# Two of GLA's eight v and gate half pieces move from the recurrences into the turns and the chunk matrices

## The reference, cut to what matters

```python
def even_mixer(x, w_in, ...):
    p = x @ w_in
    p_gla, p_rw = p[..., :GLA_IN], p[..., GLA_IN:]
    gq, gk, gv, gg, glr = jnp.split(p_gla, GLA_OFFSETS, axis=-1)      # 256, 256, 512, 512, 16 columns
    log_a = jax.nn.log_sigmoid((glr @ gla_gate_w2 + gla_gate_b)) / GLA_TAU
    o_a = gla_chunked(gq * GLA_DK ** -0.5, gk, gv, log_a)              # 4 heads
    o_a = rms_norm(o_a, gla_norm_g) * jax.nn.silu(gg)
    ...
    y = rwkv7_scan(r, decay, k, v, -kk, kk * a)                        # 8 heads
    ...
    return jnp.concatenate([o_a, o_b], axis=-1) @ w_out
```

## Time and profile before

| what | us |
|---|---|
| median of 3 runs | 1191.01 |
| lowest, highest | 1189.79, 1195.37 |
| the profiled execution | 1193.05 |
| its span in the trace | 1191.1 |
| TensorE busy in it | 1101.9 |

### The profile page before, as it was taken

One profiled execution on the slowest core, in us unless ns is written; L12 is line 12 of the kernel. 1 busy time (PEld: TensorE's weight loads), 2 busy tenths in 40 slices (PEclk: granted clock), 3 DMA queues, 4 the chain that ended last, 5 costly groups with the idle time before them and its releaser, 6 DMA issues.

```text
span 1191.1 us, 16934 instructions
## 1 busy us (share of the span) xinstructions
PE 1101.9 (93%) x7036; PEld 973.0 (82%) x7036; DVE 727.1 (61%) x1002; ACT 516.9 (43%) x734; POOL 136.8 (11%) x153
## 2 busy tenths in 40 slices
PE   5999899988999999889889899999789997999997
PEld 4798899866999988667667899998678777999885
DVE  3476875576666675745774676675655556666342
ACT  3452242244344433515663544433355656555331
POOL 1004653114000000500001300000200000000000
PEclk9897899989999999889999899999979997999999
DMA  9332002223886787254772587777434332665540
GB/s 290 107 123 73 1 2 71 72 92 120 304 278 231 249 279 251 75 175 154 107 216 83 198 284 260 248 247 283 141 123 128 105 107 72 185 194 189 195 157 36
DMA packets 113438, 193.68 MB, mean 163 GB/s; under 512 B 4658, under 2 KB 85057, under 8 KB 113234
## 3 DMA queue, kind: packets, MB, share of 16 engines
q1 hardware_dynamic: 109698, 179.66, 45.3%
q0 software_dynamic: 3248, 11.83, 4.5%
q10 hardware_dynamic: 416, 1.11, 0.2%
HBM read 188.39 MB, written 4.19 MB: 162 GB/s over the span
## 4 chain that ended last, share of the span: by engine, by line
PE 82%; DVE 9%; ACT 4%; issue 2%; SPq 1%; DMA 1%; POOL 0%; ACTq 0%; DVEq 0%
PE ps L415 22%; PE ps L416 22%; PE ps L417 22%; PE ps L1965 2%; PE ps L1950 2%; PE ps L1179 2%; DVE ARR L399 1%; PE ps L1943 1%; PE ps L1189 1%; PE ps L1416 1%; PE ps L1123 1%; PE ps L481 1%; ACT ARR L386 1%; DMA ring<-in_ffn_w_gate_up_dram 1%; DVE XL L551 1%
## 5 line engine op out<-in xcount | busy, mean ns | idle before, releaser
L399 DVE TENSOR_TENSOR ARR<-ring,ARR 128x2048 fp32r<-128x2048 f32 (+1 forms) x143 | 321.8, 2256 | 209.8 <-ACT ARR L386 209.8
L415 PE MATMUL ps<-XH,ARR 128*128 128x256 f32 x1232 | 355.9, 289 | 14.2 <-DVE XL L551 7.5
L386 ACT ACTIVATE ARR<-ring 128x2048 fp32r<-128x2048 f32 (+1 forms) x143 | 266.9, 1874 | 201.2 <-PE ps L417 141.5
L416 PE MATMUL ps<-XL,ARR 128*128 128x256 f32 x1232 | 352.9, 286 | 0.0
L417 PE MATMUL ps<-XH,ARR 128*128 128x256 f32 x1232 | 352.6, 286 | 0.0
L415 PEld LDWEIGHTS ps<-XH,ARR 128*128 128x128 f32 x1232 | 239.4, 194 | 19.7 <-issue 17.2
L416 PEld LDWEIGHTS ps<-XL,ARR 128*128 128x128 f32 x1232 | 239.4, 194 | 0.1
L417 PEld LDWEIGHTS ps<-XH,ARR 128*128 128x128 f32 x1232 | 239.3, 194 | 0.0
L415 PE MATMUL ps<-ARR 128*128 128x512 f32 x420 | 171.0, 407 | 8.8 <-DVE ARR L503 4.6
L416 PE MATMUL ps<-ARR 128*128 128x512 f32 x420 | 167.6, 399 | 0.0
L417 PE MATMUL ps<-ARR 128*128 128x512 f32 x420 | 167.4, 399 | 0.0
(11 more groups left out here) (336 smaller groups left out, 1281.9 us busy)
## 6 DMA issues: line engine op xcount, KB each, us to landing
ring<-in_ffn_w_gate_up_dram SPq DMA_DIRECT2D x44, 1024.0 KB, 5.9
ring<-in_w_dram SPq DMA_DIRECT2D x32, 1024.0 KB, 5.2
ring<-in_w_ada_dram SPq DMA_DIRECT2D x24, 1024.0 KB, 5.3
ring<-in_ffn_w_down_dram SPq DMA_DIRECT2D x22, 1024.0 KB, 5.0
ring<-in_even_w_in_dram SPq DMA_DIRECT2D x13, 1024.0 KB, 5.8
ring<-in_w_in_dram SPq DMA_DIRECT2D x9, 1024.0 KB, 5.3
ring<-in_mla_w_q_b_dram SPq DMA_DIRECT2D x6, 768.0 KB, 6.5
ring<-in_even_w_out_dram SPq DMA_DIRECT2D x4, 1024.0 KB, 5.0
```

The costliest lines, as they stand in the source:

```text
L386: e.activation(split(i)[0], raw(i), ACT.Copy).then_inc(*up("hi", ("hi", i)))
L399: e.tensor_tensor(lo, raw(i), hi.bitcast(F32), ALU.subtract).then_inc(*up("lo", ("lo", i), ("raw free", i)))
L415: e.matmul(out, lhs[0], rhs[0], start=first, stop=False)
L416: e.matmul(out, lhs[0], rhs[1], start=False, stop=False)
```

## The change

Half 0 goes into the turns and half 1 into the chunk matrices, on all three engines that touch them.

- PE: half 0 between the transposes `kb` and the product `bonus`; half 1 behind the sixth of the 16 products of the chunk matrices. In the recurrences each later half moves up, so that no half is left behind levels 3 and 5.
- ACT splits halves 0 and 1 ahead of all of the turns, and half 2 behind them. DVE does its part of halves 0 and 1 ahead of the copy of `bonus`, and half 2 where half 0 was.
- Half 1 gets a place in SBUF of its own, and both first halves wait for the last use of `qk`'s weights.
- Banks 6 and 7 are held from the turns on, so that turns, matrices and inverse go round 6 banks. DVE reads `la` after the first and second mask, no longer after the second and third.
- ACT copies v out of its banks at level 1 in place of level 3.

No instruction is added or dropped.

```diff
-        VG_SLOT = 4 * [halves(mats + 6144, 1024), (place(gg_at, 1024, of=ARR), lo_half)]
+        VG_SLOT = [halves(mats + 6144, 1024), halves(mats + 4096, 1024)] + 3 * [
+            halves(mats + 6144, 1024), (place(gg_at, 1024, of=ARR), lo_half)]
...
-            if k == 0:
+            if k < 2:
                 e.wait_ge(*at(("used", place_of["qk", 2])))
-            elif k == 1:
+            elif k == 3:
                 e.wait_ge(*at(("p done", 6, NG - 1)))
...
         def pe_turns(e):
+            banks.n = 6
...
                 k.then_inc(*up("gates", ("full", ("kb", w))))
+            pe_vg_half(e, 0)
             b = bank(e, "bonus")
...
                 k.then_inc(*up("mats", ("full", ("m", s))))
+                if s == 5:
+                    pe_vg_half(e, 1)
...
-                if s in (1, 2):
-                    t = s - 1
+                if s in (0, 1):
+                    t = s
                     e.wait_ge(*at(("abs", t)))
...
                 elif lv == 4:
-                    dve_vg_half(e, 0)
+                    dve_vg_half(e, 2)
...
                     if j == 0 and step == 4:
-                        pe_vg_half(e, 3)
+                        pe_vg_half(e, 5)
...
-        VG_BEHIND = {0: 0, 1: 1, 2: 2, 3: 4, 4: 5, 5: 6}
-        VG_SPLIT = {-1: [1], 0: [2], 1: [3], 2: [4], 3: [5, 6], 4: [7]}
+        VG_BEHIND = {0: 2, 1: 3, 2: 4, 4: 6}
+        VG_SPLIT = {-1: [3], 0: [4], 1: [5], 2: [6], 4: [7]}
 
         def pe_recurrences(e):
-            banks.n = 6
...
-                if lv == 3:
+                if lv == 1:
                     act_vg(e, 0)
...
             act_qk(e)
+            act_vg_half(e, 0)
+            act_vg_half(e, 1)
             act_turns(e)
-            act_vg_half(e, 0)
+            act_vg_half(e, 2)
...
             dve_operands(e, 3)
+            dve_vg_half(e, 0)
+            dve_vg_half(e, 1)
             dve_turns(e)
```

## The result

| | median, us | lowest to highest | runs | mean granted clock, as us at 0.50 |
|---|---|---|---|---|
| before | 1191.47 | 1189.70 to 1195.37 | 10 | 121 |
| changed | 1199.18 | 1193.52 to 1202.71 | 10 | 135 |

What follows compares the result with a forecast made beforehand. PE was taken as the bound, busy 93% of the span, with DVE's masks setting the matrices' end. Matrices +8.3 and recurrences -6.25 gave +2.05 on 1191.01, so 1193.1 us, range 1186.0 to 1199.0.

Steps and rivals of the forecast that it cites:

- Part 1: Turns: half 0 is ready behind kb, wait nought, at worst 0.2 us; bonus and the matrices start 2.90 us later.
- The bank order: Matrices: products 1 and 2 each wait for a bank round trip, 2.27 us at full clock, 3.18 at low.
- Half 1: Matrices, behind product 5: costs PE 2.90 to 5.42 us, taken as 4.1; DVE runs dry, ten masks left.
- The matrices as a whole: Turns and matrices: last mask ends at 135.3 instead of 126.99, +8.3 us; +4.4 all at full clock, +11.5 all low.
- Rival 1: Matrices: bank waits and half 1 are hidden, only half 0 is paid; -3.35, 1187.7 us; chance 0.14.
- Rival 4: Turns and matrices: half 0 or 1 not ready when PE comes, by late load or DVE; 1193.3 us; chance 0.03.
- the pairing rule: Matrices: tiles on different rows run in parallel, so products 0 and 1, a pair before, now run one after the other.
- The inverse: Inverse on six banks: costs nothing, as each bank asked for was released by an earlier step.
- Part 4: Recurrences: halves behind levels 3 and 5 go, -2.90 - 0.45 - 2.90 = -6.25 us, if the low stretch stays as long.
- rival 3: Recurrences: low clock moves onto the small products and stays, first y to half 7; +5.95, 1197.0 us; chance 0.25.
- rival 2: Matrices and recurrences: the clock stays up in both; +4.4 - 9.4 = -5.0, 1186.0 us; chance 0.13.
- the +2.05: Whole kernel: matrices +8.3 and recurrences -6.25 summed, giving 1193.1 us, counted as no change; forecast's chance 0.45.

Runs made afterwards that it cites:

- d_six_banks: Kernel before with only the changed bank order (six banks from the turns on, la read behind masks 0 and 1), no half moved: 1194.16 us, ratio 1.0042.
- a_la_early: Changed kernel with DVE's reads of la put ahead of everything else in its turns: 1192.16 us, ratio 1.0015 to the kernel before.
- i_half1_thinned: Changed kernel with half 1 cut on PE from 12 products to 2, waits and banks kept: 1196.86 us, ratio 1.0057 to the kernel before.
- c_both: Changed kernel with la read early by DVE and the six remaining halves late in the recurrences: 1190.94 us, ratio 1.0006 to the kernel before.
- b_late_slots: Changed kernel with the six remaining halves late in the recurrences, none at levels 0 and 1: 1193.72 us, ratio 1.0045 to the kernel before.
- the second trace: Changed kernel run again unchanged, for a second trace: 1198.89 us, ratio 1.0055 to the kernel before; recurrences 60.8 us in that trace.

## Why the prediction was right or wrong, point by point

**Half 0 in the turns: right.** No wait, 2.88 us for the 2.90 forecast. DVE's two steps took 2.62 us together (the earlier trace rows bounded one at 1.21 to 2.28). What Part 1 left out is the other direction: it priced what POOL does to DVE's step, and not what the step does to POOL, for which kb waits. In five of the ten traces with both steps early that is a wait of 1.00 to 2.27 us that it puts at nought, and in the three with 2.27 the clock fell in it. In the changed kernel's own two traces it is absent.

**The bank order: the mechanism right, the price right.** Two waits of 1.11 us in the changed kernel, released by the read of la, as the prediction put them. The first cycle is 2.24 us and the second 2.31, each forecast at 2.27 with the full clock and 3.18 with the low one. The clock fell one product later than I took it to, at 116.5, so the second cycle cost 2.31 and not 3.18. d_six_banks, where both fell low, shows 3.18.

**Half 1: right.** DVE idle 3.64 us (over 1 was asked for), the ten masks in one go. Half 1 took 3.71 us (121.76 to 125.47), between the two prices, forecast 4.1.

**The matrices as a whole: +7.1 for +8.3.** The end less kb's end is 24.3, forecast 25.5. The missing 1.2 is about the second cycle (0.9) and half 1 (0.4). Rival 1 (all but half 0 hidden) falls here: waits and half 1 each show their cost in the stage, in a_la_early and in i_half1_thinned. Rival 4 falls too, as neither half was late.

**What the pairing rule said.** Products alone take 1.13 us at the full clock, and 3.95 us for four in a queue at the low one, 0.99 each for 0.92 forecast; d_six_banks has 2.07 for one alone. The section "Key Properties" of "TensorEngine Tiling (Array Packing)" in the Trainium skill, which has row tiles run side by side, agrees with these rows.

**The inverse: right.** 52.51 us for 52.54. In d_six_banks and c_both it took 53.6 and 53.7, with 3.4 us more of it low; b_late_slots and i_half1_thinned had as much low and took 52.5.

**The recurrences: here the forecast failed.** Part 4 says that the low stretch lies over gp and the second y, and then: "If it stays as long, it costs as much as before". The work that left was sized well: 65.5 to 58.0 and 59.2 us in the last column of the table, a gain of 6.3 to 7.5, forecast 6.25. The clock's share was sized at nought, and it is what made the result. In the first trace the clock was at 0.50 for 28.1 us of the stage, not 6.8, which is 10.7 us more of PE's time (half of 21.3). Even rival 3, which let it stay low from the first y to half 7, still had 0.3 of the second half's 2.90 as won, put 1.3 on top, and came to -2.35 for the recurrences; this trace has +3.1. In the trace one stretch came as early as in half 5, inside level 3's step (218.90), one lies over gp, u and half 6 of level 4 (225.70), and the last, from 242.80, held through gp of level 7 and into half 7. In the second trace nothing of it came: 3.1 us. Rival 3 was right in kind, gave 1197.0, and is the nearest of the cases; rival 2 (the clock stays up) is what the second trace looks like, in which the span is 1187.8, and it is not the median.

**The sum again, with the measured terms.** Matrices +7.1, recurrences with the clock taken off -6.3 to -7.5, the gap to the mix -0.7: 0 to -1.1. On top, 11 to 14 us more at the low clock in an execution, at half speed at most 5.5 to 7. That makes +4 to +7, with 7.7 measured. Within the changed kernel's 22 runs the time rises by 0.3 to 0.4 us for each us at the low clock, by which it would be 3 to 6 (in the other kernels' runs by 0.1 to 0.5), and the sum +2 to +6. What is missing then has no measured place; the wait for POOL is a candidate. This last sum is an estimate from these figures, and where in the execution the extra low time falls isn't settled: one trace of a kernel shows one execution of it, and they differ by 25 us in one stage alone.

**The chances.** 0.79 on "within 0.5%" hung on the +2.05, and 0.63% is outside it, if barely: the interval begins at 0.47%. Since its two terms were of opposite sign and near in size, the sum stood within what the clock moves, and the clock's share pulled one way only. Putting "the low stretches vary between executions" down as a difference of the two executions' medians was the mistake behind it: I asked how long the stretches are in one trace, and not how often they come.

## What to carry to other kernels

Where PE is busy all the time, the time at the low clock is a term of its own: read it from the mean clock of all runs, and never from one trace, in which the same code took 60.8 or 72.1 us. A dense piece should go to a place where its engine waits anyway and where no order of buffers has to change for it: behind level 0 of the inverse it made no stage longer, in the turns it cost itself and two round trips. A moved piece brings its helpers along: DVE's steps beside POOL's last ones made those take 1.6 to 1.8 us in place of 0.6 to 0.8, and PE waited for them. Before taking banks from a queue, look at who frees the first one asked for; two reads of 0.41 us moved to the front were worth 5 to 6 us.

## What the runs showed of the hardware

- Stretches in which PE is busy all the time, for the most part in products of 64 or 128 columns, ran at clock 0.50 in one execution and at 1.00 in the next: 16 products of gp take 3.04 us in the one trace and 1.66 in the other, and the 438 instructions of the recurrences 72.0 and 60.7. The changed kernel's 22 runs spread from 1189 to 1207 us, and their time goes with their low time (correlation 0.83); those of the kernel before lie between 1185.4 and 1195.4. The Trainium skill, "TensorE: Matmul & The Clock Gate", section "What's actually happening", has activity lift the clock; these rows show a PE without a gap that isn't lifted.
- 12 products of 512 columns that nobody reads, 2.9 us of PE, showed no cost in the total (means 1196.6 us with, 1198.6 and 1197.7 without, standard errors 0.9 to 1.7). The low time was 7 to 10 us less, which is within about twice its error.
- Two engines at once: with a DVE operation of 128x1024 running, a POOL operation of 128x256 that started after it took 1.61 to 1.80 us in place of 0.63 to 0.82.
- A small product of half height costs 0.46 us in a queue, 1.13 alone at the full clock and 2.07 alone at the low one. A wait that breaks such a queue up costs more than its idle time.
